# Adaptive-norm modulation product moved from VectorE to the PE, in four column groups of 32

## The reference

```
c_act = silu(c)
for l in range(DEPTH):
    mod = c_act @ ada_w[l] + ada_b[l]              # 1024 -> 6 * 1024
    sh1, sc1, gt1, sh2, sc2, gt2 = split(mod, 6)
    h = rms_norm(x, norm1_g[l]) * (1 + sc1) + sh1
    x = x + gt1 * token_mixer(h, ...)               # latent attention, differential attention, convolution
    h = rms_norm(x, norm2_g[l]) * (1 + sc2) + sh2
    x = x + gt2 * conv_gated_mlp(h, w_up[l], ..., w_down[l])
return rms_norm(x, final_g)
```

## Time and profile before

| | |
|---|---|
| median of 3 runs | 1200.97 us (1198.81 to 1201.65) |
| profiled execution: its own time, the span of the trace | 1198.8 us |
| busy: PE, PEld, DVE | 87%, 82%, 78% |
| busy: ACT, POOL | 43%, 39% |
| mean granted PE clock, share of full | 0.93 |
| DMA: read, mean rate | 198.83 MB, 167 GB/s |

### The profile page before, as it was taken

One profiled execution on the slowest core, in us unless ns is written; L12 is line 12 of the kernel. 1 busy time (PEld: TensorE's weight loads), 2 busy tenths in 40 slices (PEclk: granted clock), 3 DMA queues, 4 the chain that ended last, 5 costly groups with the idle time before them and its releaser, 6 DMA issues.

```text
span 1198.8 us, 20663 instructions
## 1 busy us (share of the span) xinstructions
PE 1040.6 (87%) x7601; PEld 988.2 (82%) x7601; DVE 930.4 (78%) x1235; ACT 514.9 (43%) x715; POOL 471.6 (39%) x170
## 2 busy tenths in 40 slices
PE   2598988989788988898979898998988988889997
PEld 1498878879788988888969787887888888889996
DVE  5839898987796899888744799898788779997523
ACT  1453435526434444454335434542642454444432
POOL 5254333324443333345534433233353424444560
PEclk9798989979989999899999899987998989999998
DMA  9555332427556455556665434233665645554440
GB/s 320 197 184 166 92 116 91 158 80 256 185 191 211 140 178 179 175 205 254 239 200 173 145 116 125 90 124 115 211 212 177 213 137 175 175 178 153 166 173 36
DMA packets 138943, 201.08 MB, mean 168 GB/s; under 512 B 3416, under 2 KB 114148, under 8 KB 138852
## 3 DMA queue, kind: packets, MB, share of 16 engines
q1 hardware_dynamic: 138501, 199.63, 50.0%
q10 hardware_dynamic: 351, 0.26, 0.1%
HBM read 198.83 MB, written 1.05 MB: 167 GB/s over the span
## 4 chain that ended last, share of the span: by engine, by line
issue 58%; POOL 34%; PE 6%; DMA 1%; POOLq 0%; DVE 0%; ACT 0%; SPq 0%
POOL wL L534 33%; PE SC L1260 1%; PE SC L1262 1%; PE SC L1261 1%; DMA mask<-in_consts 1%; POOL rdev L525 0%; PE OB L1261 0%; PE OB L1260 0%; PE TR L1262 0%; PE TR L1261 0%; PE TR L1260 0%; PE OB L1262 0%; POOL ang L526 0%; POOLq L533 0%; PE ST L1228 0%
## 5 line engine op out<-in xcount | busy, mean ns | idle before, releaser
L534 POOL TENSOR_TENSOR wL<-raw,wH 128x1280 fp32r<-128x1280 f32 (+4 forms) x152 | 455.0, 3004 | 689.5 <-ACT wH L587 689.5
L1260 PE MATMUL PB<-hH,wH 128*128 128x256 f32 (+1 forms) x1568 | 476.5, 304 | 64.8 <-DVE wL L861 32.0
L1261 PE MATMUL PB<-hL,wH 128*128 128x256 f32 (+1 forms) x1568 | 458.7, 293 | 0.0
L1262 PE MATMUL PB<-hH,wL 128*128 128x256 f32 (+1 forms) x1568 | 457.9, 292 | 0.0
L1260 PEld LDWEIGHTS PB<-hH,wH 128*128 128x128 f32 (+1 forms) x1568 | 315.7, 201 | 80.5 <-issue 29.3
L587 ACT ACTIVATE wH<-raw 128x2048 fp32r<-128x2048 f32 (+3 forms) x152 | 266.3, 1769 | 134.1 <-DMA raw<-in_w_down 58.6
L1261 PEld LDWEIGHTS PB<-hL,wH 128*128 128x128 f32 (+1 forms) x1568 | 316.6, 202 | 4.1 <-issue 3.8
L1262 PEld LDWEIGHTS PB<-hH,wL 128*128 128x128 f32 (+1 forms) x1568 | 315.4, 201 | 0.0
L861 DVE TENSOR_TENSOR wL<-raw,wH 128x768 fp32r<-128x768 f32 (+4 forms) x152 | 223.9, 1475 | 98.3 <-ACT wH L587 96.1
L945 DVE SCALAR_TENSOR_TENSOR buf<-G,vec,buf 128x256 f32<-128x256 f32 x240 | 109.7, 524 | 0.3
L816 DVE SCALAR_TENSOR_TENSOR acc<-ada,c_act,acc 128x1024 f32<-128x1024 f32 x32 | 62.0, 1936 | 11.1 <-DMA ada<-in_ada_w 10.3
(11 more groups left out here) (252 smaller groups left out, 1820.9 us busy)
## 6 DMA issues: line engine op xcount, KB each, us to landing
raw<-in_w_in SPq DMA_DIRECT2D x48, 1024.0 KB, 5.6
raw<-in_w_up SPq DMA_DIRECT2D x44, 1024.0 KB, 5.1
ada<-in_ada_w SPq DMA_DIRECT2D x40, 1024.0 KB, 5.4
raw<-in_w_down SPq DMA_DIRECT2D x22, 1024.0 KB, 5.1
ada_pre<-in_ada_w SPq DMA_DIRECT2D x8, 1024.0 KB, 11.6
raw<-in_w_o SPq DMA_DIRECT2D x8, 1024.0 KB, 6.2
raw<-in_w_out_diff SPq DMA_DIRECT2D x4, 1024.0 KB, 6.4
raw<-in_w_out_conv SPq DMA_DIRECT2D x4, 1024.0 KB, 6.6
```

Source lines behind the costliest of these rows:

```text
L534: pool.tensor_tensor(wL[s][:, cut:size], raw[s][:, cut:size], wH[s][:, cut:size].bitcast(F32), ALU.subtract).then_inc(w_lo_pool[s], 1)
L1260: pe.matmul(out, a, xh(k), start=first and k == 0, stop=False, skip_group_check=True)
L1261: pe.matmul(out, a, xl(k), start=False, stop=False, skip_group_check=True)
L1262: ins = pe.matmul(out, b, xh(k), start=False, stop=last and k == kt - 1, skip_group_check=True)
```

## The change

The product moves to the PE. `c_col` holds each 128 values of silu(c) in the first of 32 columns, the other 31 zero, and is the stationary operand; the modulation weights themselves are the moving operand, float32, 512 columns at a time. The two row slabs and two column halves of a chunk go to four groups of 32 array columns, so that MI's partitions 0, 32, 64 and 96 collect four partial rows of 512. After four chunks ACT copies MI to `ada_rows` (`ada_evict`), and four matmuls with `halves` (0/1 selectors, 2 columns) add the two slabs and turn the rows to columns: four matmuls where eight stood. DVE's two passes, `acc` and its clearing go away; `ada_end` stays where it was. On the PE the product of step n now stands at the end of that step, the four of the UP loop at the end of each round, and that loop is written out on the PE.

A new product may not start in MI before DVE has read the old part from it: the first chunk of each part (steps 1, 26, 34, the first UP round, 60, 68) waits for `mi_read`, which `ada_end` gives.

```diff
-        acc = sb("acc", [P, 1024])
-        acc_pre = ada[:, 0, :]
+        ada_rows = sb("ada_rows", [P, 512])
+        c_col = sb("c_col", [P, DT, 32])
+        halves = sb("halves", [P, 2])
...
+            def ada_evict(count):
+
+                act.wait_ge(ada_used, count)
+                act.activation(ada_rows[:, :], MI[:, :], ACT.Copy).then_inc(ada_out, 1)
...
+            def ada_evict_at(l, n):
+
+                q = ADA_REDUCE_AT.get(n)
+                if q is None:
+                    return
+                if ADA_PARTS[q] < 2:
+                    with act.If(l < LAYERS - 1):
+                        ada_evict(ADA_FIRST + l * ADA_CHUNKS + ADA_PART * (q + 1))
+                else:
+                    ada_evict(ADA_FIRST + l * ADA_CHUNKS + ADA_PART * (q + 1))
...
             def mixer_step(l, n):
+                ada_evict_at(l, n)
...
+            ada_evict(ADA_PART)
             root(0, 0)
+            ada_evict(2 * ADA_PART)
             high(0, 0)
...
+                ada_evict_at(l, CHUNKS - 1)
                 squares(l + 1, 0)
...
+            link(dve.memset(halves[:, :], 0.0))
+            dve.memset(c_col[:, :, :], 0.0)
+            for q in range(4):
+                dve.memset(halves[32 * q:32 * q + 1, q % 2:q % 2 + 1], 1.0)
...
-            def ada_products(src, factor, halves, first, acc=acc):
-
-                if first:
-                    ins = dve.tensor_scalar(acc[:, :], src[:, 0, :], factor[:, 0:1], None, ALU.mult)
-                else:
-                    ins = dve.scalar_tensor_tensor(acc[:, :], src[:, 0, :], factor[:, 0:1], acc[:, :], ALU.mult, ALU.add)
-                ins.then_inc(ada_half, 1)
-                dve.wait_ge(ada_half, halves)
-                dve.scalar_tensor_tensor(acc[:, :], src[:, 1, :], factor[:, 1:2], acc[:, :], ALU.mult,
-                                         ALU.add).then_inc(ada_used, 1)
-
-            def ada_step(l, a, r=0):
-                serial = ADA_FIRST + l * ADA_CHUNKS + a + r
-                dve.wait_ge(ada_in, (l * ADA_CHUNKS + a + 1) * 16 + 16 * r)
-                if a == ADA_LOOP:
-                    dve.wait_ge(acc_clear, l + 1)
-                elif a % ADA_PART == 0:
-                    dve.wait_ge(mi_full, 2 + l * 6 + a // ADA_PART)
-                dve.wait_ge(ada_used, serial)
-                factor = c_act[:, 2, bass.ds(2 * r, 2)] if a == ADA_LOOP else factors(a % ADA_PART)
-                ada_products(ada, factor, serial + 1, a % ADA_PART == 0 and a != ADA_LOOP)
...
-            def reduce_ada(acc=acc):
-
-                for m in range(DT):
-                    ins = pe.matmul(MI[:, m:m + 1], acc[:, m * P:(m + 1) * P], ones[:, 0:1], start=True, stop=True)
+            def ada_products(src, i):
+
+                for k in range(2):
+                    for half in range(2):
+                        q = 2 * k + half
+                        ins = pe.matmul(MI[32 * q:32 * q + 32, :], c_col[:, 2 * i + k, :],
+                                        src[:, k, half * 512:(half + 1) * 512], start=(i == 0), stop=(i == ADA_PART - 1),
+                                        tile_position=(0, 32 * q), skip_group_check=True)
+                ins.then_inc(ada_used, 1)
+
+            def reduce_ada(part):
+
+                after(ada_out, part)
+                for m in range(4):
+                    ins = pe.matmul(MI[:, m:DT:4], ada_rows[:, m * P:(m + 1) * P], halves[:, :], start=True, stop=True,
+                                    skip_group_check=True)
                 ins.then_inc(mi_full, 1)
...
+            after(s_silu, 1)
             for part in range(2):
-                if part == 1:
-                    norm_sum(0, 0)
-                after(ada_used, ADA_PART * (part + 1))
                 if part:
                     after(mi_read, part)
-                reduce_ada((acc, acc_pre)[part])
+                for i in range(ADA_PART):
+                    after(ada_pre_in[ADA_PART * part + i], 16)
+                    ada_products(ada_pre[:, ADA_PART * part + i, :, :], i)
+                if part == 0:
+                    norm_sum(0, 0)
+                reduce_ada(part + 1)
...
+            def ada_step(l, a):
+
+                after(ada_in, (l * ADA_CHUNKS + a + 1) * 16)
+                if a % ADA_PART == 0:
+                    after(mi_read, l * 6 + 2 + a // ADA_PART)
+                ada_products(ada, a % ADA_PART)
+
+            def ada_at(l, n):
+
                 q = ADA_REDUCE_AT.get(n)
-                if q is None:
-                    return
-
-                def go():
-                    after(ada_used, ADA_FIRST + l * ADA_CHUNKS + ADA_PART * (q + 1))
-                    after(mi_read, l * 6 + 2 + q)
-                    reduce_ada()
-
-                if ADA_PARTS[q] < 2:
+                if q is not None and ADA_PARTS[q] < 2:
                     with pe.If(l < LAYERS - 1):
-                        go()
-                else:
-                    go()
+                        reduce_ada(l * 6 + 3 + q)
+                elif q is not None:
+                    reduce_ada(l * 6 + 3 + q)
+                a = ADA_STEPS.index(n) if n in ADA_STEPS else None
+                if a is not None and a < ADA_NEXT:
+                    ada_step(l, a)
+                elif a is not None:
+                    with pe.If(l < LAYERS - 1):
+                        ada_step(l, a)
...
-                with pe.Fori(0, UP_LOOPS) as r:
+                for r in range(UP_LOOPS):
                     for j in range(4):
                         chunk(l, UP + j, r)
+                    ada_step(l, ADA_LOOP + r)
                 for n in range(UP + 4 * UP_LOOPS, CHUNKS):
                     chunk(l, n)
-                    reduce_ada_at(l, n)
+                    ada_at(l, n)
```

More of the change, by code:

```diff
@@ L346, in trunk_kernel @@
         sc_full, e_ready = sem("sc_full"), sem("e_ready")
-        ada_in, ada_used, ada_half = sem("ada_in"), sem("ada_used"), sem("ada_half")
+        ada_in, ada_used, ada_out = sem("ada_in"), sem("ada_used"), sem("ada_rows_out")
         ada_pre_in = [sem(f"ada_pre_in{i}") for i in range(ADA_FIRST)]
-        acc_clear, v_link, p_link = sem("acc_clear"), sem("v_link"), sem("p_link")
+        v_link, p_link = sem("v_link"), sem("p_link")
         s_const, s_ones, s_xtr, s_vtr, s_vt = sem("const_made"), sem("ones_made"), sem("x_turned"), sem("vec_turned"), sem("vecs_made")
@@ L799, in _ @@
             link(dve.scalar_tensor_tensor(c_act[:, 2, :], c_act[:, 1, :], 1.0, c_act[:, 0, :], ALU.add, ALU.mult))
-            dve.tensor_scalar_mul(c_act[:, 2, :], c_act[:, 2, :], 0.5).then_inc(s_silu, 1)
+            dve.tensor_scalar_mul(c_col[:, :, 0], c_act[:, 2, :], 0.5).then_inc(s_silu, 1)
             for b in range(4):
@@ L833, in _ @@
[L833 to L838, removed]
-                             acc if a < ADA_PART else acc_pre)
-                if a == 2:
-                    dve.wait_ge(s_lam, 16)
-                    for l in range(LAYERS):
-                        ins = dve.tensor_tensor(lam_p[:, l, :, :], lam_in[:, l, 0::2, :], lam_in[:, l, 1::2, :], ALU.mult)
-                    link(ins)
-                    dve.tensor_reduce(lam_s[:, :, :], lam_p[:, :, :, :], AX.X, ALU.add).then_inc(s_lame, 1)
-                    for l in range(LAYERS):
-                        ins = dve.tensor_copy(vec_all[:, l, V_LAM:V_LAM + 2], cst[:, C_LAM + 2 * l:C_LAM + 2 * l + 2])
-                    link(ins)
-                if a == 6:
-                    dve.wait_ge(s_lamx, 1)
-                    link(dve.tensor_tensor(lamb[:, 0, :], lam_s[:, :, 1], lam_s[:, :, 0], ALU.subtract))
-                    link(dve.tensor_tensor(lamb[:, 1, :], lamb[:, 0, :], vec_all[:, :, V_LAM], ALU.subtract))
@@ new lines, in _ @@
+            dve.wait_ge(s_lam, 16)
+            for l in range(LAYERS):
+                ins = dve.tensor_tensor(lam_p[:, l, :, :], lam_in[:, l, 0::2, :], lam_in[:, l, 1::2, :], ALU.mult)
+            link(ins)
+            dve.tensor_reduce(lam_s[:, :, :], lam_p[:, :, :, :], AX.X, ALU.add).then_inc(s_lame, 1)
+            for l in range(LAYERS):
+                ins = dve.tensor_copy(vec_all[:, l, V_LAM:V_LAM + 2], cst[:, C_LAM + 2 * l:C_LAM + 2 * l + 2])
+            link(ins)
+            dve.wait_ge(s_lamx, 1)
@@ L854, in _ @@
+            link(dve.tensor_tensor(lamb[:, 0, :], lam_s[:, :, 1], lam_s[:, :, 0], ALU.subtract))
+            link(dve.tensor_tensor(lamb[:, 1, :], lamb[:, 0, :], vec_all[:, :, V_LAM], ALU.subtract))
             dve.wait_ge(s_vt, 1 + LAYERS)
@@ L1065, in ada_work @@
             def ada_work(l, n):
-                if n in ADA_STEPS:
-                    a = ADA_STEPS.index(n)
-                    if a < ADA_NEXT:
-                        ada_step(l, a)
-                    else:
-                        with dve.If(l < LAYERS - 1):
-                            ada_step(l, a)
                 for at, q in ADA_REDUCE_AT.items():
@@ L1145, in _ @@
                 norm(l, 1)
```

(4 more changed lines are left out.)

4 lines of the change are left out of this document (removed).

## The result

The changed kernel takes 1172.45 us (median of 4 runs, 1166.49 to 1174.92) beside 1199.89 us for the kernel before (1198.08 to 1201.65): a ratio of 0.9766, 95% interval 0.9737 to 0.9796. I had forecast 1231 us, slower. The rival "groups together" stood at 1176 us.

A forecast was written before the change was run, and what follows sets the result against it. DVE bounds the UP loop and parts of the mixer, PE bounds DOWN and layer heads. Start +7.5, heads +6, mixer +16, UP -16, steps 60 to 75 +18, reductions -1: +30.5, 1231 us; range 1172 to 1288.

The forecast's parts named there:

- groups together: Rival on the PE's product: all four column groups run side by side, T = 1.4 us, 1176 us; chance 0.24.
- What bounds the kernel: Whole kernel: DVE bounds the UP loop and parts of the mixer, PE bounds DOWN and the head of a layer.
- T = 2.6 us: PE time each chunk's product takes: 2.14 us of records plus 0.5 us for filling, draining and weight load.
- five slots: Chunk's product on the PE: strict start order lets only neighbouring groups overlap, five times 428 ns, 2.14 us; chance 0.45.
- lower bound of 1.4 us: Low end of a product's PE time: all four groups together, two records deep, 0.86 us, plus 0.5 us.
- The point of decision at T = 1.9: Whole kernel: the product's PE time, about 1.9 us, from which the rival with side-by-side groups decides.
- Start: Before the first main matmul: eight chunks' products on the PE delay it, +7.5 us; -3 us with groups side by side.
- Mixer and heads: Steps 24 to 40: about +8 us a layer, +16; layer heads (steps 1, 4, 7): +3 each, +6.
- UP loop: Each round: the product fills one of two 0.87 us PE gaps, 27.0 us instead of 28.96, -16 over 8 rounds.
- The new waits: PE waits for DVE's read of the old part: 4 us at step 26, 1.5 at 34, 5.1 at 60.
- Wrong if a UP round is under 26.3 us while steps 60 to 75 take less than 105: Stated failure sign, for layer 0's steps; the forecast had 27 us a round and 115.3 us for those steps.
- four starts within nanoseconds: Sign in the PE's timeline of a product that would mean the fast rival, all groups side by side.

The follow-up runs named there:

- Relief alone: The kernel before with VectorE's products cut to one column, nearly all of the product left out, nothing put on the PE: 1144.76 us, 0.9510.
- experiment 3: The changed kernel with two column groups, its product matmuls written group by group (0, 0, 1, 1) instead of in turn: 1196.74 us, 0.9952.
- At 1.93 us: The changed kernel with two column groups in place of four, each taking two of a chunk's product matmuls: ratio 0.9989 to the kernel before.
- at 1.94: The changed kernel with one extra set of four product matmuls per chunk, zero stationary operand, same groups: ratio 0.9965 to the kernel before.
- at 2.8: The changed kernel with two extra sets of product matmuls per chunk, zero stationary operand, same groups: 1236.55 us, 1.0301.
- early reads: The changed kernel with VectorE's read of the finished partial sums at the start of steps 26, 34 and 60 instead of the end: 1144.89 us, 0.9519.
- tiny products: The changed kernel with a moving operand of one column in every product matmul, so the product is left out: 1146.99 us, 0.9538.
- the moved one: The early reads kernel with each layer's first twelve products at other steps, ahead of the attention's work, and reads at 17 and 60: 1136.53 us, 0.9432.

## Why the prediction was wrong, point by point

- **What bounds the kernel: right.** VectorE bounds the UP loop; with its work gone a round falls from 28.96 to 26.34 us. Relief alone is worth 59 us.
- **T = 2.6 us: wrong, and it turned the sign.** The step was "if the PE starts matmuls in the order written ... the first record of a group can run beside the second of the group before, and no more. That makes five slots of 428 ns". The size of a slot was right (429 ns between records of the same columns); the rule was not (experiment 3): groups don't wait for each other, and so it is two slots and a T of 1.09 us. The 1.5 us too much, at 46 us for each us of T between forecast and rival, are some 69 us, more than the 59 us by which the forecast missed. Entry, exit and the uncovered weight load, 0.5 us by my estimate, are 0.2. Even my lower bound of 1.4 us was above the 1.09: it was 0.86 us for "all four groups together" and the same 0.5, and with 0.2 in its place it is the measured value. The gain that the Trainium skill gives for three column tiles ("TensorE: Matmul & The Clock Gate", Part 3: 2.38 times) would have made T 1.9; here four groups bring 3.64 / 1.09 = 3.3 times.
- **The point of decision at T = 1.9: right to a tenth.** At 1.93 us the chip gives 0.9989, at 1.94 0.9965. The rival "groups together" had the mechanism, and 1176 us for a T of 1.4. That the chip's 1172 at 1.09 lies so near is in part luck: by the slope between forecast and rival, 46 us for each us of T, 1.09 would have given some 1162. By the same slope, an estimate, steps 24 to 41 came out some 7 us dearer in the two layers and steps 42 to 59 some 10 us, and some 10 us came back where the sum had nothing: steps 0 to 7 (5.3 us), 8 to 23 (1.9) and layer 1 from step 60 on (3.1).
- **Start: right.** +9.4 us at 2.8 (forecast +7.5 at 2.6), -2.1 at 1.09 (forecast -3 for groups together).
- **Mixer and heads: near, but put too high.** The measured values at 2.8 us lie within 1.1 us a layer of the forecast's for 2.6; for 2.8 the forecast would have been 2.6 us (mixer) and 0.4 to 1.3 us (head) above them.
- **UP loop: "the product stands just there and fills one" gap of 0.87 us, wrong.** A round is 25.28 + T: 26.34 and 28.06 us, with 1.63 and 1.61 us of idle PE in them, as much as without a product (1.74 by the earlier trace rows). The PE waits there for VectorE's `wL`, 13.0 us in 16 waits, two a round. That VectorE is itself waiting for the PE's chunk, so that a product ahead of the gap only moves it, is my reading and was not followed in a trace. At 2.6 us that is 7 us too little, and does not decide the sign.
- **The new waits: places right, sizes right at 26 and 60** (3.90 and 5.43 us for 4 and 5), nearly twice the forecast at 34 (2.82 for 1.5); their price too low: 30 us with all that follows where the sum had 16, and more than the change brought in all (28 us).
- **"Wrong if a UP round is under 26.3 us while steps 60 to 75 take less than 105":** 26.34 and 102.49. The first missed by 0.04 us; the marks "four starts within nanoseconds" and VectorE below 66% (65%) were met, the PE above 90% was just missed (1048.5 of 1169.1 us, 89.7%).
- **Chances:** five slots at 0.45 against 0.24 for groups together was a choice between a rule and what the rows left open, with a slope of some 46 us for each us of T. No row excluded the fast case.

## What to carry to other kernels

Small products in separate column groups cost here as much as the deepest group, not the sum, and in both written orders that were tried: count records per group. When work leaves a busy engine for the PE, look at once for the reads by the old engine that now stand between two of the PE's steps, and put them first in their step; then put the moved work where the PE waits for the old engine, not where it used to be, and look at each place in a trace, since two badly placed products of 1.09 us cost 6 us in one layer here and 3.4 in the other.

## What the runs showed of the hardware

- A float32 product of 128 x 32 by 512 columns is two records; all four groups' first records start within some 20 ns (522.96 to 522.98 in the place shown), the second ones some 0.45 us later (523.42). Time: 0.2 us plus 0.43 us a record in the deepest group, for 2, 4, 6 and 8. With one column in place of 512 the same eight records take 0.24 us, which is the fixed part:

```profile
66.19 0.24 PE L1207 MATMUL MI<-ada,c_col 128*32 128x1 f32 x8
```

- After 5.43 and 3.90 us of idle PE the product took 1.93 and 1.94 us, after 2.82 us 1.07. The granted clock of the three stretches was 0.80, 0.84 and 0.98: two ran partly at the lower of the two levels (1.2 GHz), the third nearly all at 2.4.
- In DOWN of layer 1, where nothing was changed, 30 us hold 260 matmuls in place of 252, a chunk of 5.60 us in place of 5.76. From chunk 66 to chunk 75, before and after:

```profile
1125.41:1177.25 51.84, 51.84 (x434) 51.84 (x433) 12.35 (x9) 14.95 (x8) 30.70 (x9) 1.00 0.42 143
...
1097.36:1147.76 50.40, 50.40 (x435) 50.40 (x433) 12.49 (x9) 15.11 (x8) 30.84 (x9) 1.00 0.42 147
```

  The granted clock (1.00), the share of DMA (0.42) and the busy times of the other engines (within 0.2 us) are the same, so none of them shows a cause. It isn't the written-out loop either (with that alone, and with relief alone, steps 66 to the end of DOWN took 57.76 us as before; 56.17 in the changed kernel, with early reads and with tiny products, 56.69 in the moved one and with all products on the same columns). It is 1.6 us of the 28. In DOWN of layer 0 the matmuls lie closer too (117 ns in place of 120 in the mean). The cause stays open.
